# Products with W_out of the forgetting heads: from the norm stage into the stick-breaking steps of attention

## The reference

```python
mixed = concatenate([o_sb, o_df, o_ds, o_fx], axis=-1)
x = x + einsum('btm,md->btd', mixed, w_out)      # residual
hn = rmsnorm(x, g_ffn)                           # then a gated MLP
```

## Time and profile before

| what | value |
|---|---|
| median of 3 runs | 3651.69 us (3649.90 to 3652.66) |
| profiled execution, its own time | 3651.63 us |
| its span, first to last instruction | 3649.4 us |
| TensorE busy, share of the span | 92% |
| VectorE, ScalarE, GpSimd busy | 65%, 31%, 5% |
| mean granted clock of TensorE | 0.951 of full speed |
| attention stage of the first layer | about 554 to 964 us |
| norm stage of the first layer | about 965 to 1051 us |

### The profile page before, as it was taken

The page is one execution under the profiler, slowest core; times in us unless marked ns, Lnnn a source line. Parts: engine busy times, 40 slices in busy tenths (PEclk is TensorE's granted clock), DMA queues, the critical chain, the costliest instruction groups (busy, mean ns, idle before and its releaser), DMA issues. The chain is left out here.

```text
span 3649.4 us, 58799 instructions
## 1 busy us (share of the span) xinstructions
PE 3374.7 (92%) x21869; PEld 2930.2 (80%) x21869; DVE 2388.8 (65%) x5042; ACT 1138.8 (31%) x2363; POOL 187.5 (5%) x264
## 2 busy tenths in 40 slices
PE   5989999999969999999989899998996999999995
PEld 3978886556659999999979788765664999999994
DVE  2589994755556566565649899666475556656566
ACT  3332225555431211211142222356462121121112
POOL 1111110000000000000012111000000000000000
PEclk8999999989989999999999999999998999999997
DMA  5122233110011111111013222510100111111101
GB/s 176 43 75 82 86 110 115 62 51 13 24 47 35 52 44 42 52 39 47 12 44 99 66 73 72 183 65 20 40 27 13 55 52 43 44 52 36 50 29 49
DMA packets 228007, 211.37 MB, mean 58 GB/s; under 512 B 25382, under 2 KB 213446, under 8 KB 225758
## 3 DMA queue, kind: packets, MB, share of 16 engines
q1 hardware_dynamic: 227806, 208.72, 17.9%
HBM read 159.41 MB, written 44.91 MB: 56 GB/s over the span
## 5 line engine op out<-in xcount | busy, mean ns | idle before, releaser
L1874 PE MATMUL psum<-h_split,gate_up_split 128*128 128x352 f32 x6336 | 1020.0, 322 | 43.8 <-DVE gate_up_split L1988 43.8
L1874 PEld LDWEIGHTS psum<-h_split,gate_up_split 128*128 128x128 f32 x6336 | 1012.0, 188 | 47.9 <-issue 46.5
L2018 DVE TENSOR_TENSOR arena<-arena,psum 128x352 f32<-128x352 f32 x1056 | 513.7, 522 | 318.4 <-PE psum L1874 318.2
L1874 PE MATMUL psum<-hid_split,down_split 128*128 128x352 f32 x3168 | 523.3, 325 | 11.1 <-DVE down_split L1988 11.1
L1874 PEld LDWEIGHTS psum<-hid_split,down_split 128*128 128x128 f32 x3168 | 516.8, 190 | 11.6 <-issue 11.6
L918 PE MATMUL psum<-w_in_split,h_split 128*128 128x256 f32 x3456 | 415.5, 279 | 0.2 <-ACT arena L1049 0.2
L918 PEld LDWEIGHTS psum<-w_in_split,h_split 128*128 128x128 f32 x3456 | 402.7, 189 | 7.9 <-issue 7.4
L1190 DVE TENSOR_SCALAR_CACHE_REDUCE flags<-arena,selection 128x512 uint8<-128x512 f32 (+5 forms) x384 | 363.4, 946 | 13.7
L1746 DVE CUSTOM_DVE_ANT_0 arena<-psum,arena 128x128 f32<-128x128 f32 (+8 forms) x288 | 198.2, 704 | 169.2 <-PE psum L1518 55.0
L1959 ACT CAST hid_split<-hidden 128x1056 fp32r<-128x1056 f32 x44 | 47.3, 1076 | 834.6 <-DVE hidden L2003 834.6
L920 PEld LDWEIGHTS psum<-h_split,w_in_split 128*128 128x128 f32 x1728 | 285.2, 193 | 9.8 <-issue 9.7
(11 more groups left out here) (176 smaller groups left out, 3076.1 us busy)
## 6 DMA issues: line engine op xcount, KB each, us to landing
w_in_raw<-in_w_in SPq DMA_DIRECT2D x24, 1024.0 KB, 5.5
gate_up_raw<-in_w_gate SPq DMA_DIRECT2D x44, 512.0 KB, 3.7
gate_up_raw<-in_w_up SPq DMA_DIRECT2D x44, 512.0 KB, 4.7
down_raw<-in_w_down SPq DMA_DIRECT2D x44, 512.0 KB, 3.3
arena<-k_turned SPq DMA_DIRECT2D x8, 1184.0 KB, 5.8
k_turned<-arena SPq DMA_DIRECT2D x72, 128.0 KB, 2.1
q_turned<-arena SPq DMA_DIRECT2D x48, 176.0 KB, 1.8
arena<-bias_strips SPq DMA_DIRECT2D x4, 2048.0 KB, 10.6
```

Of the source, the lines that this page charges most:

```text
L1874: ins = nc.tensor.matmul(out, w[i], x[k], start=(first and n == 0), stop=(last and n == 2))
L2018: nc.vector.tensor_tensor(x, x, bank(m, down_bank[p])[:, 0:PIECE], ALU.add).then_inc(s.added, 1)
```

## The change

The pieces of `fx` leave the norm stage, which keeps those of `sb` alone, and run in steps 76 to 89 of the attention stage. The `ds` pieces are spread over steps 21 to 38 and those of `df` over 58 to 73. Nothing else is changed.

```diff
--- before.py
+++ after.py
@@ -1265,7 +1265,7 @@
 
 ATTEND_ORDER = ["ds", "df", "fx", "sb"]
 SLOT = dict(ds=0, df=1, fx=0, sb=1)
-FILLED = dict(ds=(21, 45), df=(60, 84))
+FILLED = dict(ds=(21, 39), df=(58, 74), fx=(76, 90))
 AHEAD = 2
 FLUSH = 5
 
@@ -2139,7 +2139,7 @@
         stage_project(nc, m, a, l, d, outs, caches, load_group("ds", 0, l))
 
         stage_attend(nc, m, a, d, l, load_group)
-        stage_norm(nc, m, 2 * FC + KC, load_gate_up(m, a, l, 0), split=True, product_of=("fx", "sb"))
+        stage_norm(nc, m, 2 * FC + KC, load_gate_up(m, a, l, 0), split=True, product_of=("sb",))
         stage_feed_forward(nc, m, a, l, (a["p_ffn_conv"][l, 0], a["s_ffn_conv"][l, 0]))
     stage_norm(nc, m, 2 * FC + 2 * KC)
     stage_store_y(nc, m, a)
```

## The result

The changed kernel takes 3670.91 us (median of 5 runs, 3668.05 to 3672.11), the kernel before 3651.23 us beside it (5 runs): a ratio of 1.0052, 95% interval 1.0038 to 1.0067. The change is slower by about 19.7 us, 9.8 a layer. The forecast was slower by 13, with 3664 us, and a range of 3648 to 3677.

The account below looks back on a forecast made before the run. TensorE, busy 92% of the span, was taken as the bound. Attention +28.0, the ds respacing +1.0 and the norm -22.5 gave +6.5 us a layer, +13 in all: 3664 us, range 3648 to 3677.

Parts of the forecast that it names:

- the sparse group: ds pieces respaced to steps 21 to 38: piece costs cancel, clock falls in emptied steps cost +1.0 us a layer.
- the norm: Norm stage: 96 fewer matmuls -28.4, wait for adds +3.9, clock fall +2.0, together -22.5 us a layer.
- late hand-over: Rival: psum banks held until VectorE leaves a scan, also in steps 80 to 85; 3682 us, half of it 3673; chance 0.17.
- signs of being wrong: Steps from 76 on growing well under 17 us, norm giving over 25, or clock falling in stretches at full level.
- Price of a piece in attention: Attention steps: a first piece costs up to 1.6 us, a second 1.2 at most; 1.1 to 1.2 taken.
- steps 76 to 85: Attention steps with fx pieces: five second pieces +5.8, four pieces in steps 84 and 85 +2.7; +8.5 us a layer.
- 60 to 75: Attention steps with df pieces: seven second pieces +7.7, steps 74 and 75 losing one each -2.1; +5.6 us a layer.
- VectorE's regime in steps 84, 85: VectorE, full there before, hides part of four new pieces: steps become 8.4 and 8.6 us, +2.7 a layer.
- the queue behind the scan in step 86: Step 86: the piece's add stands behind a VectorE scan, transposes wait 1.4 us; the step costs +2.9 us.
- slow start: Beginning of the norm at 1.2 GHz: stays, 0; could vanish, -3.0 us, if denser products before the barrier keep the clock up.
- even exchange: Rival: work moves between TensorE-bound stretches without a clock fall, +3.5 us a layer, 3659 us, other end 3646; chance 0.27.
- TensorE's room: Rival: VectorE paces the stick-breaking steps, pieces cost only their adds, 12.5 us; -10 a layer, 3632 us; chance 0.13.

Follow-up runs that it names:

- e2: Changed kernel with the norm stage as before, so the fx products are added twice: 3717.00 us, ratio 1.0182 to the kernel before.
- e3: Changed kernel with the ds pieces back in steps 21 to 44: 3659.10 us, ratio 1.0028 to the kernel before.
- e7: Changed kernel with each fx piece cut to its first chunk, adds kept: 3649.72 us, ratio 0.9998 to the kernel before.
- e10: e8 with the fx pieces moved from the norm to steps 76 to 89, df in 60 to 75: 3639.45 us, ratio 0.9962 to the kernel before.
- e5: Changed kernel with two unread matmuls of 352 columns added to each of steps 39 to 44: 3667.08 us, ratio 1.0046 to the kernel before.
- e6: Changed kernel with six unread matmuls added in the norm before its last three pieces: 3666.52 us, ratio 1.0044 to the kernel before.
- e1: Kernel before with the fx products left out of the norm and done nowhere: 3606.93 us, ratio 0.9880 to the kernel before.
- e4: Kernel before with only the ds pieces moved to steps 21 to 38: 3657.19 us, ratio 1.0022 to the kernel before.
- e8: Kernel before with ds pieces in every second step from 21 to 51 and each of 52 to 59, fx weights loaded later: 3633.07 us, ratio 0.9951.
- e9: e8 with two pieces moved from steps 52 and 53 to 22 and 24: 3635.57 us, ratio 0.9952 to the kernel before.

## Why the prediction was right, and where its sum was off

Direction and range were right: slower by more than 0.2%, inside 3648 to 3677. Its reason, that work moves from one TensorE-bound stretch into others at about its full price, is what e2, e3, e7 and e10 show. That the time came out in the range is in part luck. Two misses of opposite sign stand in the sum, the sparse group at +5.9 a layer instead of +1.0 and the norm at -24.9 instead of -22.5, and the range above 3671 was drawn from a late hand-over that did not come. Two of the prediction's own signs of being wrong did come: the clock fell in a stretch that had run at full level (steps 39 to 44, 1.00 to 0.79), and the norm gave over 25 us in the second layer.

- **Price of a piece in attention.** Second pieces at 1.1 to 1.2 us: steps 76 to 85 came out within 0.2 us of their term. So did 60 to 75, by two errors that cancel: the second pieces cost 8.3 us instead of 7.7, and steps 74 and 75 gave back 2.6 instead of 2.1. A first piece costs more than its matmuls, by 0.6 us in steps 39 to 44 (e5), where 0.34 was read from the earlier trace rows; it fits that steps 74 and 75, which lose theirs, gave back that much.
- **VectorE's regime in steps 84, 85, and the queue behind the scan in step 86.** As forecast: steps 84 and 85 take 8.39 and 8.61 us (957.34, 965.73, 974.34), forecast 8.4 and 8.6, with TensorE busy 16.65 of 17.00 us and VectorE 14.49; step 86 takes 2.77 us more, with the wait of 1.32 us in its rows. The late hand-over of banks in steps 80 to 85, a rival with 0.17, did not come: transposes wait for adds 2.6 us in all over steps 76 to 89, and 1.3 of that is step 86.
- **The norm.** The pace of adds, the wait of 3.75 us and the fall of the clock after it (1.7 us by e6) are as forecast. Where the slow start is the same on both sides, the norm gives back 22.7 us (e1, e2), so the pieces were priced right. The slow start was kept at 0 with -3.0 as the other end; the second layer took that end, the first 1.3 us of it, and so the rows show -24.9. The prediction tied that end to denser products before the barrier; e4, e8 and e9, without a piece behind step 83, start their norms just as much faster (58.18 and 59.88 us in the first layer), so nothing shows this part to be the move's.
- **The step that failed: the sparse group's pieces, +1.0.** The mechanism was named (emptied steps leave TensorE less busy, and the clock falls), the size was wrong: +7.75 and +4.14 by the rows, 4 a layer by the time of e4. I priced one fall at 1.6 us from steps 45 and 46 and allowed two of them at most, and I let the six emptied steps give back a full piece each, at a price of 1.04 that was read in a layer in which the clock happened to hold. They gave back 0.8 us in the first layer; in the second they gave back 3.9, and the steps behind them lost 3.1 of that. The rows before could have said so: steps 45 and 46, without a piece, took 11.12 us at a clock of 0.85, and 43 and 44, with two, 11.63 at 1.00, so at the fallen clock two pieces less were worth 0.5 us; and all thirteen empty steps, 45 to 57, ran at 0.73.
- **Smaller slips.** The prediction calls the adds as many as before; there are 24 more a layer, and their cost is inside the price of a piece. In the even exchange, half of the waits in the norm (3.9) and in step 86 (1.4) is 2.7 us, not 3.4, so its lower end is 3647 and not 3646.

So of +10.0 a layer by the rows, the exchange that I forecast is +4.1, the respacing +5.9; e3 and e10 have the one without the other (4.8 a layer by the time of e3, 4.5 by the rows of e10), e4 the other without the one. The rivals: TensorE's room is refuted (e2, e7), the late hand-over did not appear, and the even exchange (+3.5 a layer) describes the forgetting group's move alone quite well. It is no forecast of this change, because its condition, no fall of the clock in either stretch, does not hold.

What makes the clock fall in those steps is shown only in part. TensorE's waits in steps 39 to 44 of the changed kernel (engine, line, waited for: us in total, times, longest):

```profile
PE psum L1504 <- DVE row_mins L1746: 4.1, 3, 1.4
```

No wait is longer than 1.4 us, yet the clock is 0.79 over the 32.48 us. The Trainium skill, "TensorE: Matmul & The Clock Gate", section "A second HAM failure mode: psum-queue depth-cycling", tells of a kernel in which frequent short idle times between groups of matmuls let the clock swing between its two levels; the trace agrees with that. That added or respaced matmuls keep it up is shown (e5, e6, e8). How little a step may hold before it falls is seen in one case only: behind two neighbouring steps without a piece it fell (e9), behind single ones it held in e8 from step 39 on, and fell once for a short time in each layer of e10. Why it falls then, and whether fall and rise are regular in time, stays open.

## What to carry to other kernels

Small matmul pieces in the gaps of a loop did two things here: they used time, and they held TensorE's clock up. Six steps emptied of a piece gave back 0.8 us in the first layer instead of 7.1, and ten pieces put into empty steps cost next to nothing (e8). So read the granted clock of the steps that lose work, not only of those that gain it, and spread such pieces thinly over all steps of a loop that waits on another engine, before moving them between stages: that was worth 17.5 us here, with no work added or removed. The move between two stretches that TensorE bounds returned less than it cost, by 4 to 5 us a layer, and in step 86 the queue of the engine that adds the pieces took 1.3 us of it.

## What the runs showed of the hardware that was not expected

- Matmuls whose result nobody reads made the stretch that holds them shorter: 29.68 us with 24 more instructions, 32.48 without, and 29.68 against 30.70 in the second layer (e5).
- Pieces in every second step held the clock at 1.00 over steps 39 to 44 as pieces in every step did (e8 and the kernel before), and 3 pieces fewer took 4.0 us off.
- Ten pieces in steps 45 to 57 left the length of these steps nearly as it was, with the clock at 1.00 instead of 0.73 and 0.75: 50.10 us in both layers, against 50.53 and 48.75 without any (e8 and the kernel before).
- The slow start of the norm differed between kernels that run the same instructions from step 60 to the norm's end: the norm's 24 pieces passed in 61.20 us in the kernel before and in 58.18 in e4, whose only change lies in steps 21 to 44.
